# Keeping the split weight tiles of the first request group in DRAM for the second

## What is computed

```python
def trunk(x, mem, p):
    for i in range(DEPTH):                       # DEPTH = 2
        h = rmsnorm(x, p['norm_in'][i])
        j = i // 2
        if i % 2 == 0:                           # latent attention, 8 heads
            z = h @ p['a_w_in'][j]
            c_q, c_kv, k_r, q_mem, gate = jnp.split(z, SPLIT_A, axis=-1)
            mix = mla_mixer(c_q, c_kv, k_r, ...)  # two more projections: w_q_b, w_kv_b
        else:                                    # windowed attention, 16 heads
            z = h @ p['b_w_in'][j]
            q, k, v, q_mem, gate = jnp.split(z, SPLIT_B, axis=-1)
            mix = swa_mixer(q, k, v, ...)
        mem_o = memory_attention(q_mem, mem, ...)  # 256 memory tokens, projection w_mem_kv
        branch = jnp.concatenate([mix, mem_o], axis=-1) * jax.nn.silu(gate)
        x = x + branch @ p['w_out'][i]
    return x

y_prompt, y_sample = trunk(x_prompt, mem_prompt, p), trunk(x_sample, mem_sample, p)
```

## Time and profile before

| | before |
|---|---|
| median of 3 runs | 1382.15 us (1381.68 to 1382.49) |
| profiled execution, span | 1382.6 us |
| PE busy | 1347.7 us (97%) |
| DVE busy | 1003.1 us (73%) |
| ACT busy | 769.9 us (56%) |
| POOL busy | 417.1 us (30%) |
| granted TensorE clock, mean | 0.999 |
| DMA moved | 122.4 MB, 88 GB/s over the span |
| PE waited for other engines, in all | 31.5 us, 9.9 of them in one wait at the start |

### The profile page before, as it was taken

How to read it: one execution, slowest core, us unless ns; L and a number is a source line. 1 busy time by engine, 2 the same in 40 slices (tenths; PEclk the granted TensorE clock), 3 DMA queues, 4 the chain that set the end, 5 groups by cost and what they waited for, 6 DMA issues and landing times.

```text
span 1382.6 us, 20649 instructions
## 1 busy us (share of the span) xinstructions
PE 1347.7 (97%) x7160; PEld 1166.8 (84%) x7160; DVE 1003.1 (73%) x1964; ACT 769.9 (56%) x1719; POOL 417.1 (30%) x517
## 2 busy tenths in 40 slices
PE   6999999999999999999999999999999999999999
PEld 5789987888888889888878898888888888898887
DVE  6755588887785657888676656888887755578883
ACT  6544466555464546778554534666455554477771
POOL 1131243321012323746202213423300122437460
PEclk9999999999999999999999999999999999999999
DMA  6422321111443142212463123111123421322212
GB/s 218 130 70 64 86 83 56 41 61 37 151 145 92 41 113 87 92 54 79 152 200 104 51 79 91 64 57 51 39 81 116 137 79 52 106 85 77 70 51 99
DMA packets 80471, 122.36 MB, mean 88 GB/s; under 512 B 8305, under 2 KB 42481, under 8 KB 80369
## 3 DMA queue, kind: packets, MB, share of 16 engines
q1 hardware_dynamic: 74896, 113.35, 26.9%
q10 hardware_dynamic: 5472, 7.69, 1.8%
HBM read 116.82 MB, written 4.19 MB: 88 GB/s over the span
## 4 chain that ended last, share of the span: by engine, by line
PE 77%; DVE 12%; ACT 6%; issue 2%; DMA 1%; POOL 1%; SPq 0%; ACTq 0%; DVEq 0%; POOLq 0%
PE bank L1792 22%; PE bank L1794 22%; PE bank L1793 22%; PE bank L1837 5%; DVE w_lo_t L1087 2%; ACT prob L725 2%; PE bank L1798 2%; PE bank L1799 2%; PE bank L2143 2%; DVE probT L1094 1%; DVE part_lo L1087 1%; POOL rr L1615 1%; DVE actT L1297 1%; ACT w_hi L691 1%; DVE q_st L1151 1%
## 5 line engine op out<-in xcount | busy, mean ns | idle before, releaser
L1087 DVE TENSOR_TENSOR w_lo_t<-w_raw,w_hi 128x512 fp32r<-128x512 f32 (+3 forms) x360 | 256.0, 724 | 164.5 <-ACT w_hi L691 155.9
L691 ACT ACTIVATE w_hi<-w_raw 128x512 fp32r<-128x512 f32 (+3 forms) x360 | 214.2, 604 | 222.5 <-PE bank L1794 202.2
L1792 PE MATMUL bank<-actT,w_hi 128*128 128x512 f32 x544 | 214.8, 395 | 0.0
L1671 POOL TENSOR_TENSOR prob<-prob,rinv 128x256 f32<-128x256 f32 x192 | 138.9, 755 | 247.8 <-DVE rinv L1218 247.8
L1794 PE MATMUL bank<-actT,w_lo_t 128*128 128x512 f32 x544 | 212.2, 390 | 0.0
L1792 PE MATMUL bank<-w_hi,actT 128*128 128x512 f32 (+3 forms) x512 | 172.0, 336 | 3.9 <-DVE actT L1297 3.0
L1793 PE MATMUL bank<-w_lo_t,actT 128*128 128x512 f32 (+3 forms) x512 | 170.8, 334 | 0.0
L1794 PE MATMUL bank<-w_hi,actT 128*128 128x512 f32 (+3 forms) x512 | 170.7, 333 | 0.0
L1793 PE MATMUL bank<-actT,w_hi 128*128 128x512 f32 x384 | 149.9, 390 | 0.0
L698 ACT ACTIVATE probT<-bank 128x512 fp32r<-128x512 f32 (+1 forms) x192 | 94.8, 566 | 50.3 <-PE bank L1837 49.6
L1794 PEld LDWEIGHTS bank<-actT,w_lo_t 128*128 128x128 f32 x544 | 102.1, 188 | 21.8
(11 more groups left out here) (181 smaller groups left out, 3115.4 us busy)
## 6 DMA issues: line engine op xcount, KB each, us to landing
w_raw<-in_w_out SPq DMA_DIRECT2D x96, 256.0 KB, 2.7
w_raw<-in_w_b SPq DMA_DIRECT2D x96, 256.0 KB, 2.8
w_raw<-in_w_mem SPq DMA_DIRECT2D x64, 256.0 KB, 3.0
w_raw<-in_w_a SPq DMA_DIRECT2D x64, 256.0 KB, 2.8
bias<-in_alibi ACTq DMA_DIRECT2D x28, 192.0 KB, 2.4
w_raw<-in_w_qb SPq DMA_DIRECT2D x24, 192.0 KB, 2.3
xs<-in_x SPq DMA_DIRECT2D x8, 512.0 KB, 6.5
w_raw<-in_w_kvb SPq DMA_DIRECT2D x16, 256.0 KB, 3.3
```

Of the source, the lines that this page charges most:

```text
L691: act.activation(halves(n)[0], w_raw[:, n % RAW, 0:width], ACT.Copy).then_inc(w_hi_done, 1)
L1087: dve.tensor_tensor(halves(n)[1], w_raw[:, n % RAW, 0:width], halves(n)[0].bitcast(fp32), ALU.subtract).then_inc(w_lo_dve, 1)
L1671: pool.tensor_tensor(t, t, rinv[:, par, i:i + 1].to_broadcast(list(t.shape)), ALU.mult).then_inc(p_pool, 1)
L1792: nc.tensor.matmul(out, lhs[0], rhs[0], start=start, stop=False, skip_group_check=skip)
```

## The change

In the first group every split tile except those of `w_mem_kv` is also written to a DRAM scratch tensor `kept`, both halves, 512 KB at full width. The second group neither loads those tiles raw nor splits them: SP loads both halves from `kept` straight into the slot from which PE takes them. Of the 204 tiles of a group, 32 belong to `w_mem_kv` (8 each of `memV` and `memK` in two layers) and stay as they were; 172 are kept.

To make a kept tile one piece, the two tensors `w_hi` and `w_lo_t` become one, `w_split`, with the two halves of a slot side by side; the same holds for the second ring.

New waits: ACT's copy into a slot also waits until the slot's earlier tile has been stored (`tile_kept`), if that is a kept one. SP's load of a kept tile waits until PE has done with the slot's earlier tile (a wait that was ACT's), until that one's store is done, and until the tile itself has been stored; PE waits for the load's landing instead of DVE's remainder. The store of tile n stands on SP's queue right after the raw load of the fourth tile after it, which has itself waited for tile n's split.

```diff
+TWIN = NW // GROUPS
+KEPT = [n for n in range(TWIN) if TILES[n][0] != "mem"]
+KEPT_AT = {n: i for i, n in enumerate(KEPT)}
+AGAIN = {n + TWIN for n in KEPT}
+RAW_AT = {n: i for i, n in enumerate(n for n in range(NW) if n not in AGAIN)}
+RAW_TILES = sorted(RAW_AT)
...
-        w_hi, _ = place("w_hi", [P, SPLIT, CH], fp32r)
-        w_lo_t, _ = place("w_lo_t", [P, SPLIT, CH], fp32r)
+        w_split, _ = place("w_split", [P, SPLIT, 2, CH], fp32r)
...
             def tile_split(n):
-                eng = TILES[n][5]
-                return w_lo_dve if eng == "dve" else w_lo_pool, sum(t[5] == eng for t in TILES[:n + 1])
+                if n in AGAIN:
+                    return tile_again(n)
+                return w_lo_dve, RAW_AT[n] + 1
...
+                def keep(n):
+                    sp.dma_start(kept[KEPT_AT[n], :, :, 0:TILES[n][4]], both_halves(n).bitcast(fp32)).then_inc(tile_kept(n)[0], 16)
+
                 def load_weights(lo, hi):
                     for n in range(lo, hi):
-                        if n >= RAW:
-                            sp.wait_ge(*tile_split(n - RAW))
+                        if n in AGAIN:
+                            if ring == "extra" and n - TWIN == RING["extra"][0]:
+                                sp.wait_ge(out_done, 16 * 2 * NT)
+                            sp.wait_ge(*tile_free(before_in_slot(n)))
+                            if before_in_slot(n) in KEPT_AT:
+                                sp.wait_ge(*tile_kept(before_in_slot(n)))
+                            sp.wait_ge(*tile_kept(n - TWIN))
+                            sp.dma_start(both_halves(n).bitcast(fp32), kept[KEPT_AT[n - TWIN], :, :, 0:width]).then_inc(tile_again(n)[0], 16)
+                            continue
+                        r = RAW_AT[n]
+                        if r >= RAW:
+                            sp.wait_ge(*tile_split(RAW_TILES[r - RAW]))
...
-                        sp.dma_start(dst, src).then_inc(raw_in[n % RAW], 16)
+                        sp.dma_start(dst, src).then_inc(raw_in[r % RAW], 16)
+                        if r >= RAW and RAW_TILES[r - RAW] in KEPT_AT:
+                            keep(RAW_TILES[r - RAW])
...
                 def w_hi_to(m):
                     for n in range(count.n.get("w", 0), min(m, NW)):
-                        act.wait_ge(raw_in[n % RAW], 16 * (n // RAW + 1))
-                        if PLACE[n] >= SPLIT:
-                            act.wait_ge(*tile_free(RING[TILES[n][7]][PLACE[n] - SPLIT]))
+                        count.n["w"] = n + 1
+                        if n in AGAIN:
+                            continue
+                        act.wait_ge(raw_in[r % RAW], 16 * (r // RAW + 1))
+                        if earlier is not None:
+                            act.wait_ge(*tile_free(earlier))
+                            if earlier in KEPT_AT:
+                                act.wait_ge(*tile_kept(earlier))
...
                 def w_lo_to(m):
-                        if TILES[n][5] == "dve":
-                            dve.wait_ge(w_hi_done, n + 1)
+                        if n not in AGAIN:
+                            dve.wait_ge(w_hi_done, RAW_AT[n] + 1)
...
+    kept = nc.dram_tensor("kept_w", (len(KEPT), P, 2, CH), fp32, kind="Internal").ap()
```

More of the change, by code:

```diff
@@ L337 @@
 FIRST = {use: tiles[0] for use, tiles in CHUNKS.items()}
+TWIN = NW // GROUPS
+assert [t[:6] + t[7:] for t in TILES[:TWIN]] == [t[:6] + t[7:] for t in TILES[TWIN:]]
+KEPT = [n for n in range(TWIN) if TILES[n][0] != "mem"]
[3 more added lines that the diff above has]
+RAW_TILES = sorted(RAW_AT)
 def mem_split_count(L, k):
@@ L478, in trunk_kernel @@
             raw_in = [sem(f"raw_in{s}") for s in range(RAW)]
+            kept_out = {ring: [sem(f"kept_out_{ring}{s}") for s in range(SPLIT)] for ring in ("main", "extra")}
+            kept_in = {ring: [sem(f"kept_in_{ring}{s}") for s in range(SPLIT)] for ring in ("main", "extra")}
             w_hi_done = sem("w_hi_done")
             w_lo_dve = sem("w_lo_dve")
-            w_lo_pool = sem("w_lo_pool")
             w_used = sem("w_used")
@@ L568, in trunk_kernel, with both_halves @@
             used = {"main": w_used, "extra": part_used}
+            def both_halves(n):
+                width, ring, G = TILES[n][4], TILES[n][7], n // TWIN
+                split_of = w_split if ring == "main" else part_split[G]
+                return split_of[:, PLACE[n] % SPLIT, :, 0:width]
             def halves(n):
-                width, ring, G = TILES[n][4], TILES[n][7], n // (NW // GROUPS)
-                hi_of, lo_of = (w_hi, w_lo_t) if ring == "main" else (part_hi[G], part_lo[G])
-                return hi_of[:, PLACE[n] % SPLIT, 0:width], lo_of[:, PLACE[n] % SPLIT, 0:width]
+                return both_halves(n)[:, 0, :], both_halves(n)[:, 1, :]
             def tile_free(n):
@@ L581, in tile_free, with slot_count, tile_kept, tile_again @@
                 return used[ring], sum(t[6] is None and t[7] == ring for t in TILES[:n + 1])
-            def tile_split(n):
-                eng = TILES[n][5]
-                return w_lo_dve if eng == "dve" else w_lo_pool, sum(t[5] == eng for t in TILES[:n + 1])
+            def slot_count(n, tiles):
+                ring, slot = TILES[n][7], PLACE[n] % SPLIT
+                return slot, 16 * sum(TILES[m][7] == ring and PLACE[m] % SPLIT == slot for m in tiles if m <= n)
+            def tile_kept(n):
+                slot, value = slot_count(n, KEPT)
+                return kept_out[TILES[n][7]][slot], value
+            def tile_again(n):
+                slot, value = slot_count(n, AGAIN)
+                return kept_in[TILES[n][7]][slot], value
+            def tile_split(n):
+                if n in AGAIN:
+                    return tile_again(n)
+                return w_lo_dve, RAW_AT[n] + 1
+            def before_in_slot(n):
+                return RING[TILES[n][7]][PLACE[n] - SPLIT] if PLACE[n] >= SPLIT else None
             def half(a):
```

21 lines of the change are left out of this document (9 added, 12 removed).

## The result

After the change the kernel takes 1370.8 us (median of 4 runs, 1369.96 to 1371.46) against 1382.32 beside it; the ratio is 0.9918, interval 0.9907 to 0.993. The gain is 11.5 us. The forecast was 1375.2, a gain of 6.9, and the range ended at 1371.5: the sign was right, the size was not.

The account below looks back on a forecast made before the run. PE, busy 97% of the span, was taken as the bound. Removed waits of 7.7 us, less 0.3 for loads and 0.5 between the groups, gave 6.9 us gained: forecast 1375.2 us, range 1371.5 to 1384.

Parts of the forecast that it names:

- The ceiling: Second group, from 690 us on: PE's listed waits, 11.0 us in all, are the most that can be gained.
- the waits for remainders: Second group: PE's two waits for remainders themselves go, since both tiles come by DMA; 0.7 us gained.
- The small waits: Rotary queries, second `probT`, `qT` and smaller ones, some 2.1 us: they follow POOL or ACT work that stays; no gain.
- Layer 2's start: PE's wait for the first split activations goes whole, with ACT's first `qmem` copy and DVE's remainder; 2.2 us gained.
- Gate and residuals: Second group: 0.6 of the 1.2 us `gate` wait goes; residual (`xs`) waits give 1.1 and, for a pair, 2.3 of 2.9.
- Loads: Second group: a kept tile's load takes 3.75 us and fits its slot's window, except one gate tile, 0.3 us late.
- Nothing for these: Loads held up behind others on SP's queue, such as layer 3's raw memory tiles, and y stores: no cost.
- Stores: First group: 172 stores, 2.9 us each at 512 KB, fit the 8.2 us until slot reuse; 0.5 us lost between groups.
- A: Rival: second-group loads take longer than one alone and four slots are too few; 1380.1 us, chance 0.14.
- B: Rival: store traffic saturates DMA in the first group, loads and stores getting under 289 GB/s; 1388 us, chance 0.11.
- C: Rival: PE's waits on residuals and gates re-form over PE, ACT and DVE; 1380 us, chance 0.11.
- D: Rival: better than counted, all 11.0 us of listed waits go and nothing is added; 1371 us, chance 0.05.

Follow-up runs that it names:

- before_again: The kernel before the change, unchanged, profiled a second time: span 1380.3 us, time 1382.06 us.
- dve_sub_back: The change, with DVE making an unused two-operand SBUF subtraction at each removed remainder's place, except eight tiles of layer 2's last output chunks: 1375.10 us.
- split_again: keep_more, with ACT's slot wait and copy and DVE's dependent subtraction back in the second group, on idle slots, unused by PE: 1390.92 us.
- parts_raw: The change, but the second group's 28 `part` tiles (early output projections) are loaded raw and split as before: 1376.06 us.
- before_y_late: The kernel before the change, with the first group's last four y stores issued after 17 more weight tiles: 1380.34 us.
- dve_back: The change, with DVE making an unused one-operand reduction over a constant at each removed remainder's place in the second group: 1371.54 us.
- act_wait_back: The change, with ACT again waiting for PE to leave the slot at each removed copy's place, copying nothing: 1370.85 us.
- keep_more: The change, with layer 1's 16 memory tiles kept too and the first group's last four y stores issued after 17 more tiles: 1381.16 us.

## Why the prediction was right on the sign and short on the size

**The ceiling failed.** "That is the ceiling of the gain, unless PE runs faster for another reason; none shows." The list's 11.0 us are not all that PE loses. PE's timeline around layer 2's pause in before_again:

```profile
717.86 0.39 PE L1793 MATMUL bank<-w_lo_t,probT 128*128 128x512 f32 x1
718.09 0.39 PE L1794 MATMUL bank<-w_hi,probT 128*128 128x512 f32 x1
720.51 0.47 PE L1792 MATMUL bank<-w_hi,actT 128*128 128x512 f32 x1 [2.03 <-DVE actT L1297]
720.82 0.40 PE L1793 MATMUL bank<-w_lo_t,actT 128*128 128x512 f32 x1
721.05 0.40 PE L1794 MATMUL bank<-w_hi,actT 128*128 128x512 f32 x1
```

The list counts from 718.09 + 0.39 to 720.51: 2.03. But the next matmul would have started 0.23 after the last, at 718.32: 2.19 are lost, and the first matmul after the pause keeps the second waiting 0.31 instead of 0.23. Each pause costs some 0.25 more than listed, and one below 0.16 isn't listed. Before has 14 in the list, so the ceiling was about 11.0 + 14 x 0.25 = 14.5 (an estimate), and the end of the range, 1371.5, which stood on it, was too high. The rule was at hand, that a matmul takes up the distance to the next start and not its printed time; I applied it to the matmuls and not to the pauses. It made probT 1.1 instead of 0.8, the xs at 1299 1.6 instead of 1.1, and the waits for remainders 1.9 in three instead of 0.7 in two (the third, at 737, was hidden in the first trace: its slow matmuls brought PE there later).

**The small waits failed.** "The other waits ... follow POOL or ACT work that stays, and I leave them." Listed at 1.5 without the second probT, which stayed, they brought 3.0 us, the largest part of the 4.7 or so by which the removed side was short. What stood nearest to the wait stays, but the remainders before it don't: dve_sub_back brought back 0.5 each at 889 and 891 and 0.4 to 0.5 at 915 and 959 with DVE's time alone. The prediction priced a remainder at 0.69 and read the 2.39 us for two as a cost, without asking why these two took so long: POOL was at work beside them, and both engines got slower. So POOL's work stays, but its length didn't. 1266 returned only with the whole chain of all tiles (split_again), 1308 already with that of the `part` tiles (parts_raw).

**Layer 2's start** came out at 2.2, less 0.3 for the second tile, as counted, but by another cause: not the copy and the remainder, but a tile that landed late (before_y_late). The prediction followed the chain back to ACT and stopped there, so that the size came out as counted was in part luck: the kept tiles are loaded among the same y stores, and the second one was 0.3 late.

**Gate and residuals** held: 0.6 for 0.6, 2.2 for 2.3 at the pair of residuals.

**Loads** held: 3.9 us in the median for 3.75. The bQ tile that "just fits" was 0.2 late, the gate tile behind aQ was on time within 0.1 in after (in the traces of dve_back, act_wait_back, parts_raw and dve_sub_back 0.2 to 0.6 late, near the forecast's 0.3), and the second qmem tile, not foreseen, 0.3 late among y stores. "Nothing for these" on the raw tiles of layer 3 was off by 0.4.

**Stores** held in sum: no cost from 60 to 684 us, 0.4 for 0.5 between the groups. A store took 4.9 us in the median where 2.9 had been counted, which the 8.2 us until the slot's next use hid. That is the 2 us more that the prediction had tried against itself; whether the write's completion or the loads beside it took them isn't shown.

**Rivals.** A showed only in the bQ tile's 0.2. B did not decide here, but keep_more crossed its bound and lost 8 us: the bound was real, and it is a matter of bytes per microsecond of PE's work on a tile. C didn't occur. D named the right time, 1371, by the wrong sum: not all listed waits went, and some 1.0 us was added between 686 and 1178; the pauses were worth more than listed.

The first trace's own time had to be its span and 1.76 us around it (after: 1369.96 for a span of 1368.2), so that execution was 2.2 us above the median and not 0.45. The forecast, a gain taken from the median, doesn't change by it, but the first trace holds about 2 us of slow matmuls that are not in every execution; those at the start are no matter of this change, and those behind the pause can go only with the pause.

## What to carry to other kernels

When PE is the bound, add up pauses as start-to-start distance less the steady one, not as listed idle time, and count the small ones: what precedes the last step before a wait counts as much as that step. Price an instruction by its rows at that place, since beside POOL a subtraction took 1.79 us here instead of 0.68, and rebuild it with the same operands in an experiment. Work that is replaced by memory traffic is free only where bytes per tile over PE's time on that tile stay below what the DMA gives.

## What was not expected of the hardware

A subtraction over 512 columns on DVE with two SBUF operands took 1.79 us when it began during POOL's instruction and 0.68 when it began before it; two reductions with one operand took 1.26 together at the same place; POOL's instruction went from 1.30 to 1.68. After a pause of 1.9 to 2.2 us at the same place two executions ran eight matmuls at a granted clock of 0.51 and a third, whose pause of 2.0 lay between theirs, ran on at 1.00. Loads and stores together moved 355 and 414 GB/s at a full share, more than the 350 and 299 of the earlier trace rows.
